# Forming the merge-gate weight sums on GpSimd in place of VectorE, and two operands at the output projection's end

## The reference

```python
hproj = x @ w_in[l]
...
g_na, g_ml = jnp.split(jax.nn.sigmoid(merge_g), 2, axis=-1)
mixed = g_na * (y_na @ w_branch_na[l]) + g_ml * (y_ml @ w_branch_ml[l])
x = layer_norm(DEEPNORM_ALPHA * x + mixed @ w_out[l], ln1_g[l], ln1_b[l])
f = conv_glu(x, ffn_w_up[l], ffn_conv_w[l], ffn_conv_b[l], ffn_w_down[l])
```

## Time and profile before

| | us |
|---|---|
| median of 3 runs (2717.52 to 2719.61) | 2719.13 |
| profiled execution, its own time | 2718.12 |
| span of the profile | 2716.6 |
| PE busy | 2656.7 (98%) |
| DVE busy | 2086.7 (77%) |
| ACT busy | 1387.9 (51%) |
| POOL busy | 271.7 (10%) |

### The profile page before, as it was taken

How to read it: one execution, slowest core, us unless ns; L and a number is a source line. 1 busy time by engine, 2 the same in 40 slices (tenths; PEclk the granted TensorE clock), 3 DMA queues, 4 the chain that set the end, 5 groups by cost and what they waited for, 6 DMA issues and landing times.

```text
span 2716.6 us, 37235 instructions
## 1 busy us (share of the span) xinstructions
PE 2656.7 (98%) x13797; PEld 2261.0 (83%) x13797; DVE 2086.7 (77%) x2697; ACT 1387.9 (51%) x1879; POOL 271.7 (10%) x349
## 2 busy tenths in 40 slices
PE   8999999999999999999979999999999999999996
PEld 7888888888888888888867888888888888888885
DVE  5455354576687777558897999999999987888888
ACT  4444444444455555334465666566666664444444
POOL 2000001100110000011011111111111001000000
PEclk9999999999999999999989999999999999999998
DMA  5333333333477766688626777777777678357453
GB/s 166 98 97 85 97 97 93 99 88 95 109 182 154 172 149 183 222 285 323 225 83 148 189 185 203 211 199 181 210 201 205 167 195 345 140 196 268 156 193 108
DMA packets 502489, 461.97 MB, mean 170 GB/s; under 512 B 16072, under 2 KB 442364, under 8 KB 497600
## 3 DMA queue, kind: packets, MB, share of 16 engines
q1 hardware_dynamic: 407712, 309.44, 36.9%
q0 software_dynamic: 91440, 145.26, 21.5%
q10 hardware_dynamic: 3184, 5.24, 0.6%
HBM read 383.30 MB, written 76.59 MB: 169 GB/s over the span
## 4 chain that ended last, share of the span: by engine, by line
PE 92%; DVE 6%; ACT 1%; issue 1%; DMA 0%; ACTq 0%; DVEq 0%; SPq 0%
PE ps L2695 20%; PE ps L2697 11%; PE ps L2358 10%; PE ps L2360 10%; PE ps L2359 10%; PE ps L2593 7%; PE ps L2646 6%; PE ps L2648 6%; PE ps L2647 6%; PE ps L2594 4%; PE ps L2352 1%; DVE aop L2074 1%; PE ps L2573 1%; PE ps L2553 0%; DVE dw L1924 0%
## 5 line engine op out<-in xcount | busy, mean ns | idle before, releaser
L2695 PE MATMUL ps<-aop,uw 128*128 128x512 f32 x2408 | 608.2, 394 | 6.2 <-DVE aop L2074 5.7
L2695 PEld LDWEIGHTS ps<-aop,uw 128*128 128x128 f32 x2408 | 434.8, 190 | 84.4 <-DVE aop L2074 6.4
L1470 DVE TENSOR_TENSOR wlo<-raw,whi 128x512 fp32r<-128x512 f32 x288 | 197.6, 690 | 335.7 <-ACT whi L909 328.9
L909 ACT ACTIVATE whi<-raw 128x512 fp32r<-128x512 f32 x288 | 179.8, 629 | 464.2 <-PE ps L2360 458.3
L1924 DVE TENSOR_TENSOR uw<-quad,uw 128x1024 fp32r<-128x1024 f32 x301 | 367.7, 1222 | 55.9 <-ACT uw L1256 54.3
L1256 ACT ACTIVATE uw<-quad 128x1024 fp32r<-128x1024 f32 x301 | 318.0, 1056 | 85.1 <-PE ps L2697 75.1
L2358 PE MATMUL ps<-x_hl,whi 128*128 128x512 f32 x896 | 354.3, 395 | 1.8 <-DVE wlo L1470 1.8
L2697 PEld LDWEIGHTS ps<-aop,uw 128*128 128x128 f32 x2408 | 331.6, 191 | 24.6
L2360 PE MATMUL ps<-x_hl,wlo 128*128 128x512 f32 x896 | 349.4, 390 | 0.0
L2359 PE MATMUL ps<-x_hl,whi 128*128 128x512 f32 x896 | 349.3, 390 | 0.0
L2697 PE MATMUL ps<-aop,uw 128*128 128x256 f32 x2408 | 338.7, 283 | 0.0
(11 more groups left out here) (337 smaller groups left out, 4400.6 us busy)
## 6 DMA issues: line engine op xcount, KB each, us to landing
quad<-in_ffn_w_up SPq DMA_DIRECT2D x172, 512.0 KB, 3.8
raw<-in_w_in SPq DMA_DIRECT2D x224, 256.0 KB, 2.8
region<-in_ffn_w_down SPq DMA_DIRECT2D x32, 1280.0 KB, 9.7
a_dram<-ah SPq DMA_DIRECT2D x20, 1792.0 KB, 9.1
aopb<-a_dram POOLq DMA_DIRECT2D x28, 1280.0 KB, 7.2
gq<-in_w_in SPq DMA_DIRECT2D x63, 512.0 KB, 3.7
quad<-in_ffn_w_up POOLq DMA_DIRECT2D x43, 512.0 KB, 6.7
w_region<-in_w_out SPq DMA_DIRECT2D x16, 1024.0 KB, 8.5
```

What stands on the lines that cost most here:

```text
L1470: nc.vector.tensor_tensor(wlo[:, k % HL, :], raw[:, k % RAW, :], whi[:, k % HL, :].bitcast(F32), ALU.subtract).then_inc(w_lo_ready, 1)
L2695: return mm(ps[:, bank, :], uw[:, n % 3, 0, k, :], a.rearrange("p h t -> p (h t)"), start=i < 2 and k == 0, stop=False, skip_group_check=True)
```

## The change

`gate_form` moves from DVE to POOL with its operations and waits, and waits in addition for the low parts that read the tiles it overwrites. POOL's order is new: the three sums of step 0 stand behind `add_upper(1)`, those of step 1 behind `add_upper(2)`, and from step 2 on the first sum stands before `add_upper(step + 1)` and the other two behind it. At the output projection's end `operand_lo(N_W + 1)` and `form(0, 1)` move from DVE to POOL, behind the DMA that accumulates q11's weights onto q12.

```diff
+            def gate_form(step, j):
+                pool.wait_ge(s["g_lo"], FROM["g_lo"] + 7 * step + (2, 1, 3)[j - 1])
+                q11, q12, q21, q22 = [gate_quad(step, q) for q in range(4)]
+                if j == 1:
+                    pool.wait_ge(gq_in[step % 2][3], gq_count(step))
+                    pool.wait_ge(gt1_in[step % 2], gq_count(step))
...
+                    ins = nc.gpsimd.tensor_tensor(q12, q12, q22, ALU.add)
+                elif j == 2:
...
+                    ins = nc.gpsimd.tensor_tensor(q11, q11, q12, ALU.subtract)
+                else:
...
+                    ins = nc.gpsimd.tensor_tensor(q12, q12, q21, ALU.add)
+                ins.then_inc(s["g_formed"], 1)
             add_upper(0)
             store_pair(3, 0)
             add_upper(1)
+            for j in (1, 2, 3):
+                gate_form(0, j)
             add_upper(2)
+            for j in (1, 2, 3):
+                gate_form(1, j)
             store_pair(3, 1)
...
-            for step in range(3, KB):
-                add_upper(step)
+            for step in range(2, KB):
+                gate_form(step, 1)
+                if step + 1 < KB:
+                    add_upper(step + 1)
+                for j in (2, 3):
+                    gate_form(step, j)
...
+            n, q12 = N_W + 1, quad[0][1][:, :, :]
+            pool.wait_ge(t1_in[0], quad_count(0))
+            pool.wait_ge(s["op_hi"], n + 1)
+            pool.wait_ge(s["op_lo"], n)
+            nc.gpsimd.tensor_tensor(uw[:, n % 3, 1, :, :], q12, uw[:, n % 3, 0, :, :].bitcast(F32), ALU.subtract).then_inc(s["op_lo"], 1)
+            pool.wait_ge(quad_in[0][3], quad_count(0))
+            nc.gpsimd.tensor_tensor(q12, q12, quad[0][3][:, :, :], ALU.add).then_inc(s["t_formed"], 1)
...
-                    if i in (1, 2, 3):
-                        gate_form(step, i)
...
-            operand_lo(N_W + 1)
-            form(0, 1)
```

More of the change, by code:

```diff
@@ L743, in add_upper @@
                                accum_op=ALU.add).then_inc(gt1_in[step % 2], 16)
+            def gate_form(step, j):
[4 more added lines that the diff above has]
+                    pool.wait_ge(gt1_in[step % 2], gq_count(step))
+                    if step == 1:
+                        pool.wait_ge(s["r_in"], 16 * ML_H + 16)
+                    ins = nc.gpsimd.tensor_tensor(q12, q12, q22, ALU.add)
+                elif j == 2:
+                    pool.wait_ge(gq_in[step % 2][0], gq_count(step))
+                    pool.wait_ge(s["g_formed"], FROM["g_formed"] + 3 * step + 1)
+                    ins = nc.gpsimd.tensor_tensor(q11, q11, q12, ALU.subtract)
+                else:
+                    pool.wait_ge(gq_in[step % 2][2], gq_count(step))
+                    pool.wait_ge(s["g_formed"], FROM["g_formed"] + 3 * step + 2)
+                    ins = nc.gpsimd.tensor_tensor(q12, q12, q21, ALU.add)
+                ins.then_inc(s["g_formed"], 1)
             add_upper(0)
@@ L1775, in _ @@
                 na_units(ub, 2, plus(softmax(i, 0, 0), {7: [lambda: gate_lo(0)]} if i == 3 else {}, both(i, 1)))
[L1777 to L1794, removed]
             def ml_c22(step):
```

## The result

The changed kernel takes **2750.47 us** (median of 5 runs, 2748.85 to 2752.85) against 2719.13 us (5 runs, 2717.17 to 2721.57) before: ratio 1.0117, 95% interval 1.0106 to 1.0128. It is slower by 31.3 us, where 11.5 was forecast, and lies 10 us beyond the forecast's range. The profiled execution has 2750.47 us itself, with a span of 2748.9.

What follows compares the result with a forecast made beforehand. PE was taken to bound the settled steps, DVE only the gate stage's start and the output projection's end. 10.8 + 2.4 + 0.6 - 2.3 = +11.5 us on 2718.1 gave 2729.6, with the median 1.0 above: 2730.6 us, range 2724 to 2740.

Steps and rivals of the forecast that it cites:

- the slow sum: Rival: a sum on POOL is far slower, so every step waits from 3.7 us per sum; about 2765 us, chance 0.05.
- The long stall: Step 1: the first sum stands behind add_upper(2) and its late quadrant; PE idles 9.4 us before product 9, +10.8 us.
- The clock: After the stop before product 9, PE's clock falls to the 1.2 GHz level for one product: +2.4 us, floor 0.
- the projection's end: End of the output projection: two instructions leave DVE's queue between the statistics and c21_w, which starts 2.28 us earlier: -2.3 us.
- The settled steps: nothing.: Settled gate steps: PE covers DVE and the later sums on POOL are still in time, so cost 0.
- D: Time of one sum on POOL, taken as 2.3 us against 1.22 on DVE; floor 0.91, ceiling 2.74.
- The hold-up: Rival: DVE's and POOL's two-input instructions hold each other up, at the start and in settled steps; 2733.7 to 2737.7 us, chance 0.25.
- The start: Steps 0 and 1 until product 9: late softmax, then the stall behind add_upper(2), +10.8 us in all.
- The softmax's end: Step 0: POOL's late first sum delays DVE's softmax, so shifted(1) ends at 770.2 in place of 768.2, +2.0 us.
- the rival's 2.2: Start, engines holding each other up: gate_lo(2) waits 1.2 us and the mask 1.0, so shifted(1) ends 2.2 us later; chance 0.25.
- the late first sum: Step 2: its first sum stands behind store_pair(3, 1) and the loads of y_raw, delaying a product: +0.6 us.
- the likeliest case: The forecast itself, whole kernel: +11.5 us, 2730.6 us, own range 2727 to 2732, chance 0.55.

Runs made afterwards that it cites:

- e2: Changed kernel with step 1's three sums ahead of add_upper(2) in POOL's queue; 2741.15 us, ratio 1.0077.
- e1: Kernel before with only the change's second part: at the output projection's end POOL makes the operand's low part and first weight sum; 2716.22 us, ratio 0.9988.
- e3: Changed kernel with add_upper(step + 1) behind the third sum from step 2 on; 2736.11 us, ratio 1.0059.
- e4: Changed kernel, same order, but from step 2 on the second sum waits for the low part of the step's product 2; 2735.28 us, ratio 1.0059.
- e9: Changed kernel with a 128x1024 memset on POOL between add_upper's issue and the second sum in steps 2 to 14; 2763.53 us, ratio 1.0165.
- e11: e9 with one more wait, for the memset's own semaphore, between the memset and the second sum; 2735.13 us, ratio 1.0057.
- the last profile: Changed kernel with e2's and e3's orders, step 0's first sum before add_upper(1), and steps 0 and 1's second sum waiting for the second low part; 2724.31 us.

## Why the prediction was right in sign and too small

**Right, and right in size.** A sum on POOL takes 2.33 to 2.42 us where it is alone (forecast 2.3), so the slow sum is ruled out. The long stall is there, for the reason given: 8.69 us without work on PE (forecast 9.4), the quadrant landing 9.9 us behind its release (9.2), and e2 takes 9.3 us away by moving one line. The clock cost 2.2 us (2.4), at 0.50 in the window of 791 to 796, which is the 1.2 GHz level. At the projection's end the two instructions between the statistics and `c21_w` are gone (2.28 us forecast): 1.8 us by the two profiles, 2.3 by e1's, and 3.0 as a whole program (e1, with an interval of 0.8 to 5.7).

**The step that failed: "The settled steps: nothing."** It says "Cost 0 for D up to 3.7", and the steps cost 14.2 us. D was within that bound; e3 and e4 show that the sums' length and their late times cost nothing there (period 19.55 us with them). What costs is that they shut DVE out. The hold-up was a rival with a chance of 0.25, and its place in settled steps was even named, but priced at "up to 0.3 us per step": it was 1.18. Two things were wrong in that price. I took the hold-up to last as long as the two engines' recorded times overlap, and the second sum to start behind its issue, at a time that leaves the low part alone. In fact the sum behind an issue holds DVE before the issue has ended (3.91 us in place of 1.22), and e9 with e11 show that a queued add does so before it is on record itself. And I compared sums of busy time (10.7 + 6.9 us against 19.55) where the low parts have due times: PE waits 0.89 us for the one that is late, although DVE has idle time elsewhere in the step.

**The start: +3.1 more than forecast.** The softmax's end came 4.4 us late where 2.0 was forecast. The low part (2.50 for 1.22 us) and the mask (2.20 for 1.22) are held, 2.3 us together, close to the rival's 2.2. Nearly all of the other 0.7 us is the quadrant's transfer: `add_upper(2)` issued 9.9 us behind the softmax's end (773.85 to 783.77) in place of 9.3. Behind product 9's clock came another 3.5 in place of 0.6, and step 2 holds all of it: 0.7 for the late first sum, as forecast, and 2.8 for held low parts. Most of the latter goes with e4's wait (step 2 takes 20.91 us there).

**Taken together** the mechanism with the sign was right, and the likeliest case left out a cost that a rival had named. With that rival in the sum and the settled steps at 1.18 each in place of 0.3, it would be 2733.7 + 14.2 = 2747.9.

## What to carry to other kernels

Moving two-input work from VectorE to GpSimd isn't free of VectorE: while a GpSimd add reads SBUF, a VectorE instruction with two SBUF inputs stands still, if the add was at work or already queued when it started. Price the move by which of VectorE's instructions the adds will meet, and by those instructions' due times, not by busy shares. Keep an add away from the place right behind a DMA issue or another GpSimd instruction with no wait between: put it elsewhere, or have it wait for the VectorE instruction that it would hold up. And where an engine has slack (here VectorE under a PE that never idles), relieving it gives nothing; the 3 us that this change gave were at the projection's end, where VectorE's queue was the path.

## What the runs showed of the hardware

- **A queued GpSimd add holds VectorE before it is on record.** VectorE's subtraction started 0.65 us (with a memset between issue and add) and 0.41 us (behind two issues) ahead of the add, and lasted 4.79 and 4.99 us in place of 1.22. With a wait between the memset and the add it lasted 1.23. How far back the hold can reach is open, and so is what the engine does then.
- **GpSimd's next instruction is on record about 0.95 us behind the start of a DMA issue that is itself on record for 1.55**: 836.90 against 835.93 and, for a memset, 902.67 against 901.75.
- **Writes don't hold VectorE up**: 108 memsets of 1.03 us, 0.0% (0.999 to 1.0009).
- **A scaling with one matrix input is held too**: the four TENSOR_SCALAR of 128x256 in the last profile lasted 4.97 us beside two adds, in place of 1.14; two of the four took 2.03 and 2.49 us, the others 0.34. By the Trainium skill (SBUF — State Buffer, Who interferes with whom) `tensor_scalar` can enter a mode that takes the shared pair; the row agrees, though no run here isolates it.
- **A reduction isn't held**: in that profile the TENSOR_REDUCE of 128x1024 at 758.26 runs beside an add (757.30 to 760.48) and takes its 1.22 us, while the TENSOR_SCALAR behind it takes 1.00 us in place of 0.17.
- **The clock fell after a stop of only 3.09 us as well.** PE waited until 765.06, and the granted clock was 0.66 in the next five microseconds. The product that began at 766.65 took 3.86 us in place of 2.87. The forecast had put this cost behind the long stall alone.

```profile
760.00:765.00 5.00, 1.97 (x10) 1.29 (x8) 4.90 (x6) 1.09 (x5) 1.33 (x1) 1.00 0.00 0
765.00:770.00 5.00, 4.94 (x20) 4.33 (x21) 4.92 (x10) 3.36 (x8) 0.00 (x0) 0.66 0.00 0
```
